# Gating and norms placed beside matrix products, and three additions put into evictions, in a three-block single-core kernel

## The reference

```python
m = jax.nn.sigmoid(g_a) * ya + jax.nn.sigmoid(g_b) * yb      # yb = gated @ w_b + b_b
y = m @ w_out + b_out
x = _layer_norm(DEEPNORM_ALPHA * x + g1 * y, post1_g[l], post1_b[l])
h = _layer_norm(x) * (1 + sc2) + sh2
y = _moe(h, ...)
x = _layer_norm(DEEPNORM_ALPHA * x + g2 * y, post2_g[l], post2_b[l])
```

```python
proj = h @ w_in[l]
z, xbc, dt_raw, q, f_fwd, f_bwd, i, g = jnp.split(proj, IN_SPLITS, axis=-1)
# state-space mixer:  y_ssd = rmsnorm_3(y * silu(z), norm_w)      over all 1024 channels
# recurrence:         y_hg  = rmsnorm_3(y, norm_w) * silu(g)      over the 128 channels of a head
y = jnp.concatenate([y_ssd, y_hg], axis=-1) @ w_out[l]
x = x + gate1 * y
```

## Time and profile before

| | us |
|---|---|
| median of 3 runs (4509.75 to 4515.1) | 4512.72 |
| the profiled execution, whole | 4505.31 |
| its span, first to last instruction | 4503.5 |
| TensorE busy | 3737.5 |
| VectorE busy | 1381.8 |
| ScalarE busy | 698.2 |

### The profile page before, as it was taken

How to read it: one execution, slowest core, us unless ns; L and a number is a source line. 1 busy time by engine, 2 the same in 40 slices (tenths; PEclk the granted TensorE clock), 3 DMA queues, 4 the chain that set the end, 5 groups by cost and what they waited for, 6 DMA issues and landing times. The chain is left out here.

```text
span 4503.5 us, 32149 instructions
## 1 busy us (share of the span) xinstructions
PE 3737.5 (83%) x11618; PEld 1804.1 (40%) x11618; DVE 1381.8 (31%) x2445; ACT 698.2 (16%) x1295; POOL 225.3 (5%) x241
## 2 busy tenths in 40 slices
PE   6976667799878499999999997694699667589998
PEld 2524233344343144444444443243344556334444
DVE  0015422239221411211112112327533577511011
ACT  1021110101110210100001000312252233110000
POOL 0000000210000100000000001000000444000000
PEclk8985557899999699999999998896799888899999
DMA  2211631462110599999999996112222000212221
GB/s 77 68 58 50 228 130 43 144 226 82 56 48 19 230 365 403 400 409 400 400 407 401 409 400 220 56 38 72 83 75 75 5 5 1 75 56 75 75 75 37
DMA packets 219296, 729.49 MB, mean 162 GB/s; under 512 B 16208, under 2 KB 27105, under 8 KB 184375
## 3 DMA queue, kind: packets, MB, share of 16 engines
q1 hardware_dynamic: 179132, 629.94, 37.0%
q10 hardware_dynamic: 28394, 55.66, 3.5%
q0 software_dynamic: 11664, 42.47, 2.7%
HBM read 678.33 MB, written 49.69 MB: 162 GB/s over the span
## 5 line engine op out<-in xcount | busy, mean ns | idle before, releaser
L1623 PE MATMUL bank<-moe_gu,all_hT 128*128 128x512 f32 x1088 | 471.9, 594 | 0.0
L1117 PE MATMUL bank<-all_hT,early_w 128*128 128x512 f32 x896 | 390.0, 598 | 22.6 <-PEq L135 11.7
L1813 DVE TENSOR_TENSOR all_hT<-bank,moe_bias 128x512 f32<-128x512 f32 x51 | 35.3, 692 | 971.9 <-PE bank L1623 682.4
L1623 PEld LDWEIGHTS bank<-moe_gu,all_hT 128*128 128x128 f32 x1088 | 207.5, 191 | 261.1 <-issue 261.1
L1649 PE MATMUL bank<-moe_dn,moe_rows 128*128 128x512 f32 x544 | 265.7, 651 | 44.6 <-DMA moe_dn<-in_w_dn_dram 43.7
L1117 PEld LDWEIGHTS bank<-all_hT,early_w 128*128 128x128 f32 x896 | 171.9, 192 | 240.7 <-issue 240.7
L1636 PE MATMUL bank<-moe_gu,all_hT 128*64 128x512 f32 x1088 | 236.5, 592 | 1.0 <-issue 1.0
L2590 PE MATMUL bank<-hg_qs,hg_ks 128*128 128x128 f32 x896 | 138.3, 302 | 115.6 <-DVE hg_ks L2562 113.8
L1117 PE MATMUL bank<-all_hT,late_w 128*128 128x512 f32 x512 | 221.9, 596 | 12.1 <-PEq L135 12.1
L2334 PE MATMUL bank<-all_hT,hin_w 128*128 128x512 f32 x512 | 222.7, 598 | 9.9 <-PEq L372 9.9
L1117 PE MATMUL bank<-b_up,late_w 128*128 128x512 f32 x512 | 220.0, 592 | 1.7 <-PEq L1089 1.7
(11 more groups left out here) (533 smaller groups left out, 4095.6 us busy)
## 6 DMA issues: line engine op xcount, KB each, us to landing
moe_gu<-in_w_gu_dram SPq DMA_DIRECT2D x136, 2048.0 KB, 21.1
moe_dn<-in_w_dn_dram SPq DMA_DIRECT2D x68, 2048.0 KB, 22.9
early_w<-in_w_in_dram SPq DMA_DIRECT2D x13, 2048.0 KB, 9.0
expert_rows<-conv_zeros POOLq DMA_DIRECT2D x49, 512.0 KB, 17.2
early_w<-in_w_mod_dram SPq DMA_DIRECT2D x12, 2048.0 KB, 8.1
early_w<-in_ada_w_dram SPq DMA_DIRECT2D x12, 2048.0 KB, 7.9
hin_w<-in_w_in_dram SPq DMA_DIRECT2D x10, 2048.0 KB, 8.4
late_w<-in_w_up_dram SPq DMA_DIRECT2D x8, 2048.0 KB, 9.0
```

Source lines behind the costliest of these rows:

```text
L1117: mm = nc.tensor.matmul(B[b][:], w[:, k, m * P:(m + 1) * P], src[:, i * KT + k if stacked else k, :], start=(k == 0), stop=(k == KT - 1))
L1623: mm = nc.tensor.matmul(B[bank][:], xb2[:, k, :], gu[:, q, kk, col:col + HALF], start=(k == 0), stop=(k == KT - 1))
L1813: after(vec.tensor_tensor(g, gate[:], bias[0], ALU.add), 1)
```

## The change

Four blocks of the program go away (`add_tiles` three times, `multiply_tiles`), and so do the blocks of n10 and of `hgrn_norm` as separate stages. The additions "m" and "r" are made in the evictions of `wb` and `wo`, one dependent VectorE instruction after the first. The addition "x2" is made in `combine`, on VectorE, tile by tile behind ScalarE's copies. Gate and norm of `y_ssd` move into `hgrn_inputs`, and the per-head norm and the product "wo3" become one block, `mixed_out`. The first loads of `hin` and `late` are issued at the start of those two blocks. Seven semaphores are added in `hgrn_inputs`, one in `mixed_out`, two in `second_mixer`, and those of the blocks that are gone drop out; after n11 the count of used ones is 80 instead of 84, so that the clearing falls between "up" and "down" instead of ahead of "up".

```diff
-        linear(core, core.early, "wb", 1, tile(2), gated_product(5, c["b_b"]))
-        add_tiles(core, "m", tile(4), tile(5))
...
-        linear(core, core.early, "wo", 1, tile(4), ("vector", emit))
-        add_tiles(core, "r", xT, tile(0), ALPHA)
...
+        def add_product(i, b, bank):
+            nc.vector.scalar_tensor_tensor(out=tile(5)[:, b, :], in0=bank[:], scalar=c["b_b"][:, b:b + 1],
+                                           in1=tile(5)[:, b, :], op0=ALU.add, op1=ALU.mult).then_inc(other_gated, 1)
+            nc.vector.wait_ge(other_gated, b + 1)
+            return nc.vector.tensor_tensor(tile(4)[:, b, :], tile(4)[:, b, :], tile(5)[:, b, :], ALU.add)
+
+        def add_branch(i, b, bank):
+            nc.vector.tensor_scalar(tile(0)[:, b, :], bank[:], c["b_out"][:, b:b + 1], mod[:, 16 + b:17 + b],
+                                    ALU.add, ALU.mult).then_inc(branch_gated, 1)
+            nc.vector.wait_ge(branch_gated, b + 1)
+            return nc.vector.scalar_tensor_tensor(out=xT[:, b, :], in0=xT[:, b, :], scalar=ALPHA, in1=tile(0)[:, b, :],
+                                                  op0=ALU.mult, op1=ALU.add)
+
+        linear(core, core.early, "wb", 1, tile(2), ("vector", add_product))
+        linear(core, core.early, "wo", 1, tile(4), ("vector", add_branch))
...
 def combine(core, rows_dram, row, weight, share, ident, b_dn, gain, acc, xT):
...
         @block.vector
...
+            for k in range(KT):
+                dve.wait_ge(copied, k + 1)
+                nc.vector.scalar_tensor_tensor(out=xT[:, k, :], in0=xT[:, k, :], scalar=ALPHA, in1=acc[:, k, :],
+                                               op0=ALU.mult, op1=ALU.add).then_inc(added, 1)
...
 def hgrn_inputs(core, stream, hT, f, q, gate, v_tm, kh, total, lower, y_ssd, zs, ssd_gain, ones):
...
         @block.tensor
...
+                        if i == 0 and n == 4:
+                            for k in range(KT):
+                                pe.wait_ge(squared, k + 1)
+                                mm = nc.tensor.matmul(B[7][:], ones[:], squares[:, k, :], start=(k == 0),
+                                                      stop=(k == KT - 1))
+                            mm.then_inc(square_summed, 1)
+                        if i == 0 and n == 7:
+                            pe.wait_ge(std_ready, 1)
...
         @block.scalar
...
-            for n in range(8):
+            for k in range(KT):
+                act.wait_ge(gated, k + 1)
+                func(squares[:, k, :], y_ssd[:, k, :], ACT.Square).then_inc(squared, 1)
+            for n in range(4):
+                take(FORGET, n, f[0][:, n, :], ACT.Identity)
+            act.wait_ge(eps_set, 1)
+            act.wait_ge(square_summed, 1)
+            func(rstd[:], B[7][:], ACT.Sqrt, bias=eps_col[:], scale=1.0 / D).then_inc(std_ready, 1)
+            for n in range(4, 8):
                 take(FORGET, n, f[0][:, n, :], ACT.Identity)
...
         @block.vector
...
+            for k in range(KT):
+                vec.tensor_tensor(y_ssd[:, k, :], y_ssd[:, k, :], zs[:, k, :], ALU.mult).then_inc(gated, 1)
+            dve.wait_ge(std_ready, 1)
+            vec.reciprocal(rstd[:], rstd[:]).then_inc(inverted, 1)
+            dve.wait_ge(inverted, 1)
+            dve.wait_ge(gated, KT)
+            for k in range(KT):
+                vec.scalar_tensor_tensor(out=y_ssd[:, k, :], in0=y_ssd[:, k, :], scalar=ssd_gain[:, k:k + 1], in1=rstd[:],
+                                         op0=ALU.mult, op1=ALU.mult).then_inc(ssd_normed, 1)
...
-def hgrn_norm(core, stream, y, out, gain, gate, ones, scratch):
+def mixed_out(core, stream, y, y_ssd, y_hg, gain, gate, ones, scratch, xT, scale):
...
-            stream.load(sp, 0)
+            stream.load(sp, 4)
...
-            for k in range(HG_H):
-                pe.wait_ge(squared, k + 1)
-                nc.tensor.matmul(B[k][:], ones[:], scratch[:, k, :], start=True, stop=True).then_inc(summed, 1)
+            def sums(first):
+                for k in range(first, first + 4):
+                    pe.wait_ge(squared, k + 1)
+                    if first:
+                        pe.wait_ge(rooted, k - 3)
+                    nc.tensor.matmul(B[4 + k % 4][:], ones[:], scratch[:, k, :], start=True, stop=True).then_inc(summed, 1)
+
+            for i, src in enumerate((y_ssd, y_hg)):
+                for s in range(2):
+                    w = stream.take(pe)
+                    for m in range(4):
+                        n = 4 * s + m
+                        if i:
+                            pe.wait_ge(added, n + 1)
+                        elif s:
+                            pe.wait_ge(rooted, HG_H)
+                        for k in range(KT):
+                            if i and n == 0:
+                                pe.wait_ge(done, k + 1)
+                            mm = nc.tensor.matmul(B[n][:], w[:, k, m * P:(m + 1) * P], src[:, k, :], start=(k == 0),
+                                                  stop=(k == KT - 1))
+                        mm.then_inc(stream.product, 1)
+                        if i == 0 and n < 2:
+                            sums(4 * n)
...
         @block.vector
...
+            def add(n):
+                b = n % 8
+                dve.wait_ge(stream.product, base + n + 1)
+                if n >= 8:
+                    dve.wait_ge(added, b + 1)
+                nc.vector.scalar_tensor_tensor(out=xT[:, b, :], in0=B[b][:], scalar=scale[:, b:b + 1], in1=xT[:, b, :],
+                                               op0=ALU.mult, op1=ALU.add).then_inc(added, 1)
+
+            for k in range(HG_H):
+                head(k)
+            for n in range(16):
+                add(n)
...
-                multiply_tiles(core, hin, "z", y_ssd, zs)
-                norm(core, "n10", y_ssd, y_ssd, ones, y_hg, c["ssd_norm_w"])
...
-                hgrn_norm(core, late, hT, y_hg, c["hg_norm_w"], gs, ones, hq)
+                mixed_out(core, late, hT, y_ssd, y_hg, c["hg_norm_w"], gs, ones, hq, xT, mod[:, 16:24])
...
-            linear(core, late, "wo3", 2, ycat, add_gated(16), stacked=True)
```

More of the change, by code:

```diff
@@ L1831, in _, with combine @@
                 step_units(i, False)
-def combine(core, rows_dram, row, weight, share, ident, b_dn, gain, acc):
+def combine(core, rows_dram, row, weight, share, ident, b_dn, gain, acc, xT):
     nc = core.nc
@@ L2277, in _, with hgrn_inputs @@
                 mm.then_inc(pair_done, 1)
-def multiply_tiles(core, stream, name, x, y):
-    nc = core.nc
-    with ExitStack() as ctx:
-        (done,) = sems(nc, ctx, f"multiplied_{name}")
-        block = ctx.enter_context(nc.Block())
-        @block.sync
-        def _(sp):
-            stream.load(sp, 0)
-        @block.vector
-        def _(dve):
-            for k in range(x.shape[1]):
-                nc.vector.tensor_tensor(x[:, k, :], x[:, k, :], y[:, k, :], ALU.mult).then_inc(done, 1)
-def hgrn_inputs(core, stream, hT, f, q, gate, v_tm, kh, total, lower):
+def hgrn_inputs(core, stream, hT, f, q, gate, v_tm, kh, total, lower, y_ssd, zs, ssd_gain, ones):
     nc = core.nc
@@ L2305, in hgrn_inputs @@
     with ExitStack() as ctx:
-        reset, diff = bufs(nc, ctx, "hgate", reset=[P, T], diff=[P, 2 * KT])
+        reset, diff, rstd, eps_col = bufs(nc, ctx, "hgate", reset=[P, T], diff=[P, 2 * KT], rstd=[P, T], eps=[P, 1])
+        squares = v_tm.rearrange("p t (a c) -> p (t a) c", a=2)
+        eps_set, gated, squared, square_summed, std_ready, inverted, ssd_normed = sems(
+            nc, ctx, *(f"ssd_{s}" for s in ("eps_set", "gated", "squared", "square_summed", "std", "inverted", "normed")))
         (copied, loaded, diffed, magnitude, rate, log_term, kept, outer_magnitude, outer_rate, outer_term, log_sig,
@@ L2320, in _ @@
             stream.load(sp, 10)
+        @block.gpsimd
+        def _(pool):
+            nc.gpsimd.memset(eps_col[:], EPS).then_inc(eps_set, 1)
         @block.tensor
@@ L2639, in hgrn_norm @@
         (eps_col,) = bufs(nc, ctx, "hn", eps=[P, 1])
-        eps_set, squared, summed, rooted, inverted, normed, done = sems(
-            nc, ctx, *(f"hn_{s}" for s in ("eps", "squared", "summed", "rooted", "inverted", "normed", "done")))
+        eps_set, squared, summed, rooted, inverted, normed, done, added = sems(
+            nc, ctx, *(f"hn_{s}" for s in ("eps", "squared", "summed", "rooted", "inverted", "normed", "done", "added")))
         block = ctx.enter_context(nc.Block())
+        base = stream.base()
         @block.sync
         def _(sp):
-            stream.load(sp, 0)
+            stream.load(sp, 4)
         @block.gpsimd
@@ L2663, in _, with head @@
         def _(pe):
-            for k in range(HG_H):
-                pe.wait_ge(squared, k + 1)
-                nc.tensor.matmul(B[k][:], ones[:], scratch[:, k, :], start=True, stop=True).then_inc(summed, 1)
+            def sums(first):
[21 more added lines that the diff above has]
+                            sums(4 * n)
         @block.vector
```

(2 more changed lines are left out.)

32 lines of the change are left out of this document (9 added, 23 removed).

## The result

| | before | after |
|---|---|---|
| median of the runs compared, us | 4511.24 (4509.06 to 4515.1, 4 runs) | 4445.91 (4438.63 to 4452.12, 4 runs) |
| ratio, 95% interval | 1 | 0.9854 [0.9837, 0.9871] |
| the profiled execution, us | 4505.31 | 4447.54 |
| its span, us | 4503.5 | 4445.7 |

The change makes the kernel faster by 1.5%. The forecast was 4455.4 with a range of 4446 to 4468; the median lies 0.09 us under the range. The profiled execution, for which the sum was made, was forecast at 4448.0 and came out at 4447.54: 57.8 us saved where the sum said 57.3. That these two agree so closely is partly luck: the same two kernels profiled again (4504.98 and 4454.40, in the experiments) lie 50.6 apart.

The account below looks back on a forecast made before the run. TensorE, 83% busy, was taken as the bound, held by barriers at five idle stretches. Terms 4.5 + 4.5 + 4.4 + 9.5 + 30.3, clock +5.8 and -1.7, gave 57.3: 4512.7 - 57.3 = 4455.4 us, range 4446 to 4468.

Parts of the forecast that it names:

- m and r, clock at wo and n6 included: Before wo and n6, additions hidden beside matmuls save 4.5 us each; full clock there returns 2.8 and 3.0 more.
- x2: Before n8, each addition follows its ScalarE copy in combine, so TensorE starts 4.4 us earlier.
- gate and norm of y_ssd: At hgrn_inputs, TensorE starts 16.3 us earlier, less 6.87 for sums between banks: net 9.5 us.
- heads and wo3: In mixed_out, heads hide beside the first product pass; start 37.2 us earlier, less 6.87 for sums: net 30.3.
- clearing's clock at "down": Between "up" and "down", clearing semaphores lengthens the idle time to 3.0 us; lower clock costs 1.7, bounds 0 and 2.8.
- The clock at wo: At wo, after idle time cut to about 1.8 us, the clock stays full, returning 2.8 us.
- The second rival: At the bare loads, first pieces land after 14.3 us: 12.2 lost, 45.1 saved, 4467.6 us; chance 0.08.
- the third (heads not hidden): In mixed_out, slower heads hold the second pass; at double cost 27 us late, 4482.4 us; chance 0.03.
- the fourth (low clock in mixed_out): In mixed_out, products get the low clock, 6.87 us more per bank, 109.9 over 16: 4565.3 us; chance 0.01.
- The clock at n6: At n6, after about 1.9 us idle, no clock loss was expected, returning 3.0 us.
- The first rival: At wo and n6, the clock does not come back: 51.5 us saved instead of 57.3, 4461.2 us; chance 0.24.
- the median of the runs is 7.4 above that execution: Whole kernel: 7.4 us between profiled execution and median, taking the forecast from 4448.0 to 4455.4 us.

Follow-up runs that it names:

- after_again: The changed kernel, with no edit, run and profiled again: ratio to before 0.9867, median 4449.71 us.
- only_gate: The kernel before with only the gate and norm of y_ssd moved into hgrn_inputs: ratio 0.9985, median 4499.19 us.
- before_again: The kernel before, with no edit, run and profiled again beside itself: ratio 1.0001, median 4507.41 us.
- only_additions_m_r: The kernel before with only the additions m and r put into the evictions: ratio 0.9964, median 4491.11 us.
- sums_first: The changed kernel with the ones-matrix matmuls moved ahead of the first bank in hgrn_inputs and mixed_out: ratio to before 0.9847, 4437.86 us.
- sums_first_quarters: The changed kernel with ones-matrix matmuls ahead of the first bank and the first piece of hin and late in four loads: ratio to before 0.9832, 4427.85 us.
- sums_first_again: The same kernel as sums_first, measured and profiled a second time: ratio to before 0.9838, median 4432.72 us.
- reciprocal_twice: The changed kernel with a second, unread reciprocal in every head of mixed_out: ratio to before 0.9919, median 4469.35 us.

## Why the prediction was right or wrong

**The sum.** Point by point, forecast and the stages measured:

| term | forecast, us | measured, us |
|---|---|---|
| m and r, clock at wo and n6 included | 4.5 + 4.5 + 2.8 + 3.0 = 14.8 | 151.9 - 140.1 = 11.8 and 10.16 - 8.80 = 1.4: 13.2 |
| x2 | 4.4 | stage 3.1 (alone), 3.7 and 4.0; last copy to n8 5.5 - 1.2 = 4.3 |
| gate and norm of y_ssd | 9.5 | 9.0 (alone), 10.4 and 11.3 |
| heads and wo3 | 30.3 | 30.25 (alone), 29.75 and 29.75 |
| clearing's clock at "down" | -1.7 | 0 at "down"; from n11 to the end -0.5 |
| sum | 57.3 | 57.4 (after), 56.9 (after_again) |

(The stage up to n6 ends at the block's start, so the clock's loss inside n6 is outside it. The gate's stage is 304.5 less 293.2 in after; only_gate gives 304.3 less 295.3. Two numbers are for after and after_again.)

The two profiled executions of the first pair lie 57.8 apart, because the stages that the change doesn't touch differ by only 0.4 in sum there; those of the second pair (before_again less after_again, spans) lie 50.5 apart, because there the untouched stages take 6.3 more, the recurrence alone 5.5. So the sum by stages is right within 1 us twice, and that one profiled execution came out within 0.5 of its forecast is luck on top.

**Right.** m and r: TensorE starts 1.01 us after the last addition began (1392.63 less 1391.62), and the forecast said 0.69 + 0.31. The wait that the change adds costs 0.03 us: 0.78 from start to start for an instruction of 0.75. The clock at wo came back in full; the 2.8 us that the sum has for it are the 9.93 of the first 16 records less 7.13, and the runs show the same over all 128, 57.99 less 55.17. x2 as forecast. The first landing at hgrn_inputs was forecast 9.5 us after the block's start and came at 9.06; the sums stood in the path for 6.87 and no gap followed at bank 7. In mixed_out the first head began 20.5 us after the block's start (forecast 22.6), the last ended at 58.8 (60.8), the second pass began at 72.5 (72.0), the last eviction at 127.5 (126.9). Two small slips in the working didn't matter: an eighth of 14.3 - 8.7 + 0.4 is 0.75 and not 0.65, and the 256 KB in front of the first weights cost next to nothing (8.6 and 8.7 us from issue to landing in the two profiles of the changed kernel and 8.7 in before, though 9.4 in only_gate). The second rival (slower landings), the third (heads not hidden) and the fourth (low clock in mixed_out) did not come about: landings of 8 to 9 us, 13 us to spare, clock 1.00. 629.94 of the 729.49 MB of the kernel before went over one queue, q1 (page, parts 2 and 3), and the longest landing of a piece of hin was 14.3 us there and 14.5 in after, but the first piece kept its 8 to 9.

**Wrong in size, in both directions.** The clock at n6 was taken as coming back whole, 3.0; it came back by 1.4, and in every kernel with this part (8.80 us in after, after_again and only_additions_m_r, each after 1.90 us idle). The first rival was thus half true at n6 and false at wo, and the clock below 1.00 at n6 (0.69) is one of the signs that the prediction itself named against it. I had chosen the rows with 1.68 and 1.98 us as the nearest, and idle time alone doesn't decide it. The loss charged at "down" (1.7) wasn't there in the changed kernel, though TensorE stood for 2.78 us before it:

```profile
4196.51 219.97 PE L1117 MATMUL bank<-b_up,late_w 128*128 128x512 f32 x512 [2.78 <-PEq L135]
```

That is the timeline of after; the 512 records take 219.97 us, and in a profile of the kernel before also 219.97, after 1.68. These two misses, -1.6 and +1.7, cancel, and that is luck. The gate gave 0.5 less than forecast alone and 0.9 and 1.8 more in the two whole kernels. Most of that follows how slowly TensorE starts after its wait for the weights: the first eviction began 9.69 us after the first matmul in the kernel before, 9.95 in only_gate, 9.36 in after_again and 8.58 in after (3214.10 less 3205.52), with the clock at 0.73 over 3237.5 to 3247 in the kernel before and 0.84 over 3205.5 to 3214.5 in after, where eight matmuls at full clock take 6.87. The rest is the first landing, forecast 9.5 us after the block's start and measured 9.8 in only_gate and 9.1 in the other two.

**The step that failed** is the last of the sum: "the median of the runs is 7.4 above that execution, so 4512.7 - 57.3 = 4455.4". It took the offset of one profiled execution to the median of three runs as a property of the kernel. The runs show that it is none: before_again puts the same program at 4506.4 to 4507.4 with a profiled execution of 4505.0, and over the 13 profiles the offset runs from -4.7 to +10.2. For the changed kernel it was -1.6. Of the 9.5 us by which the forecast missed, 7.4 are the offset added, 1.6 the one found and 0.5 the sum. Without it the forecast is the profiled execution's own, 4448.0, which is 2.1 us above the median measured and 1.7 below that of after_again. How much of the 7.4 is scatter of single executions and how much a difference between sets of runs stays open, as said above. There also failed "each case is good to 3 us or so", taken from three runs' spread of 5.4: single executions of one kernel lie up to 21 us apart, and medians of four runs of the changed kernel differ by 3.8 (4445.91, 4449.71). With 6 us of scatter on both sides the low bound is 4443 even from the forecast as it was put, and the result is inside; that is said with the result known. The bounds were also not quite the sums named for them: 4455.4 - 1.7 - 4 - 3 is 4446.7, and 4461.2 + 6.1 + 3 is 4470.3, not 4468. And 0.09 us under the range is itself no more than chance: the same kernel measured again, 4449.71, lies in it.

What stays open: the difference of the medians is 65.3 in the first comparison (4511.24, 4445.91) and 56.7 in the other (4506.39, 4449.71), so some us of it don't belong to the change; whether the true figure is nearer 57 or 65 the timed runs don't settle, though the stages, 56.9 and 57.4, speak for the lower end. They lie just under what both intervals allow, so a gain of an us or more that no stage shows isn't excluded. The intervals, 0.9837 to 0.9871 and 0.9852 to 0.9882, share 0.9852 to 0.9871, that is 58 to 67 us.

## What to carry to other kernels

Where a barrier holds TensorE while another engine works alone, price the move as the whole idle time less what stays on the path: the first weights' landing (9.1 and 8.2 us here), and every matmul that has to stand between banks (6.87 us for eight). Matmuls that are ready before the weights belong into the wait for them, and that alone gave another 15 to 16 us of the two stages here, 2.4 of which were lost again at n11 and "down". Put a forecast on many runs, never on a median of three, test its terms stage by stage, and let the range hold the scatter between executions beside the doubt in the terms.

## What the runs showed of the hardware that I had not expected

The same short idle time costs clock in one kernel and not in another. At n11 and at "down" it did so again when the kernel was profiled again. Timeline of sums_first, TensorE, at n11 and at "down":

```profile
3932.72 8.83 PE L397 MATMUL bank<-b_up,all_ones 128*128 128x512 f32 x16 [1.98 <-ACT b_up L426]
...
4177.41 221.67 PE L1117 MATMUL bank<-b_up,late_w 128*128 128x512 f32 x512 [2.78 <-PEq L135]
```

And of sums_first_quarters, the same two places:

```profile
3933.74 7.13 PE L408 MATMUL bank<-b_up,all_ones 128*128 128x512 f32 x16 [1.98 <-ACT b_up L437]
...
4176.46 219.97 PE L1128 MATMUL bank<-b_up,late_w 128*128 128x512 f32 x512 [1.68 <-PEq L1100]
```

After 1.98 us at n11 eight matmuls take 7.13 us in ten of the profiles and 8.83 in those of sums_first, sums_first_again and reciprocal_twice. After 2.78 us at "down" the 512 records take 219.97 in after and after_again, and 221.67 in the same three. Each time the difference is 1.7 us. In sums_first the clock is 0.81 over 3932.7 to 3941.6 and 0.82 over 4177.4 to 4187, in sums_first_quarters 1.00 over 3933.7 to 3940.9 and over 4176.4 to 4186.4. Idle for 1.83 or 1.84 us at wo, the engine lost nothing in any of the eight profiles with that part; idle for 1.89 or 1.90 at n6, it lost 1.7 in all eight. Before wb it stands for 2.42 or 2.43 us, after short products, and lost nothing in any of the 13 (128 records in 55.17). And the program doesn't decide it either: at the sums of mixed_out, after 1.99 us both times, eight matmuls took 7.13 in sums_first and 8.83 in sums_first_again, as shown above. Between 1.8 and 2.8 us the length of the idle time thus doesn't tell whether the clock falls. What does, these runs don't say.
